# Hybrid attention and state-space layer, fp32 on one core: first tile of x in two column halves, last row tile's final product in two halves of 256 columns

## What is computed

```python
xn = rmsnorm(h, norm1_w[layer])
proj = xn @ w_in[layer]
...
h = h + mix.astype(h.dtype)
hn = rmsnorm(h, norm2_w[layer])
u = causal_dwconv(hn @ w_up[layer], ffn_conv_w[layer], ffn_conv_b[layer])
val, gt = _split(u, (D_FF, D_FF))
h = h + ((jax.nn.silu(gt) * val) @ w_down[layer]).astype(h.dtype)
return rmsnorm(h, final_norm_w)
```

## Time and profile before

| what | us |
|---|---|
| median of 3 runs | 1033.05 |
| lowest, highest | 1031.88, 1033.41 |
| the profiled execution | 1032.09 |
| its span, first to last instruction | 1030.4 |
| PE busy in it | 1020.3 |
| PEld busy | 832.3 |
| DVE busy | 642.4 |
| ACT busy | 465.9 |
| POOL busy | 93.6 |

### The profile page before, as it was taken

One profiled execution on the slowest core, in us unless ns is written; L12 is line 12 of the kernel. 1 busy time (PEld: TensorE's weight loads), 2 busy tenths in 40 slices (PEclk: granted clock), 3 DMA queues, 4 the chain that ended last, 5 costly groups with the idle time before them and its releaser, 6 DMA issues.

```text
span 1030.4 us, 13442 instructions
## 1 busy us (share of the span) xinstructions
PE 1020.3 (99%) x5095; PEld 832.3 (81%) x5095; DVE 642.4 (62%) x897; ACT 465.9 (45%) x834; POOL 93.6 (9%) x128
## 2 busy tenths in 40 slices
PE   9999999999999999999999999999999999999997
PEld 8887777777888888888888888898888888888886
DVE  7637998684476686895754544566766676641332
ACT  6335556455555636765633222444444444331233
POOL 0001111110222120122220100000000000000000
PEclk9999999999999999999999999999999999999999
DMA  7622221224656424555362743223332223232222
GB/s 218 123 85 82 82 69 55 83 82 114 160 122 168 130 84 128 141 128 150 102 211 83 253 156 104 80 83 104 100 119 85 81 84 120 89 129 89 93 71 81
DMA packets 123499, 116.49 MB, mean 113 GB/s; under 512 B 21342, under 2 KB 111782, under 8 KB 123447
## 3 DMA queue, kind: packets, MB, share of 16 engines
q1 hardware_dynamic: 95509, 94.74, 29.9%
q10 hardware_dynamic: 25346, 12.59, 5.3%
q0 software_dynamic: 2592, 8.46, 2.2%
HBM read 109.41 MB, written 6.36 MB: 112 GB/s over the span
## 4 chain that ended last, share of the span: by engine, by line
PE 87%; DVE 9%; ACT 2%; issue 1%; DMA 0%; SPq 0%; DVEq 0%; ACTq 0%
PE banks L1270 27%; PE banks L1271 26%; PE banks L1272 26%; DVE conv_acc L1218 3%; DVE w_lo L871 1%; PE banks L1375 1%; PE banks L1368 1%; ACT probs L622 1%; PE banks L1363 1%; PE banks L1343 1%; PE banks L1351 1%; DVE probs L963 1%; DVE small L949 0%; DVE scores L946 0%; DMA w_raw<-in_w_in 0%
## 5 line engine op out<-in xcount | busy, mean ns | idle before, releaser
L871 DVE TENSOR_TENSOR w_lo<-w_raw,w_hi 128x1024 fp32r<-128x1024 f32 (+1 forms) x166 | 201.4, 1253 | 124.0 <-ACT w_hi L584 122.8
L584 ACT ACTIVATE w_hi<-w_raw 128x1024 fp32r<-128x1024 f32 (+1 forms) x166 | 164.1, 1037 | 108.9 <-PE banks L1272 107.6
L1270 PE MATMUL banks<-xn_hi,w_hi 128*128 128x512 f32 x528 | 211.8, 401 | 0.0
L1271 PE MATMUL banks<-xn_lo,w_hi 128*128 128x512 f32 x528 | 206.1, 390 | 0.0
L1272 PE MATMUL banks<-xn_hi,w_lo 128*128 128x512 f32 x528 | 206.0, 390 | 0.0
L1270 PE MATMUL banks<-hn_hi,w_hi 128*128 128x512 f32 (+1 forms) x376 | 141.3, 376 | 0.0
L1271 PE MATMUL banks<-hn_lo,w_hi 128*128 128x512 f32 (+1 forms) x376 | 141.2, 375 | 0.0
L1272 PE MATMUL banks<-hn_hi,w_lo 128*128 128x512 f32 (+1 forms) x376 | 141.2, 375 | 0.0
L1270 PEld LDWEIGHTS banks<-xn_hi,w_hi 128*128 128x128 f32 x528 | 99.1, 188 | 29.8 <-issue 9.3
L1272 PEld LDWEIGHTS banks<-xn_hi,w_lo 128*128 128x128 f32 x528 | 99.1, 188 | 21.6
L1271 PEld LDWEIGHTS banks<-xn_lo,w_hi 128*128 128x128 f32 x528 | 99.3, 188 | 18.9
(11 more groups left out here) (222 smaller groups left out, 1460.0 us busy)
## 6 DMA issues: line engine op xcount, KB each, us to landing
w_raw<-in_w_in SPq DMA_DIRECT2D x29, 1024.0 KB, 5.4
w_raw<-in_w_up SPq DMA_DIRECT2D x22, 1024.0 KB, 5.0
decay<-acs_scratch ACTq DMA_DIRECT2D x16, 512.0 KB, 6.1
w_raw<-in_w_ssd_o SPq DMA_DIRECT2D x8, 1024.0 KB, 5.3
w_raw<-in_w_down SPq DMA_DIRECT2D x8, 1024.0 KB, 5.0
w_raw<-in_w_in SPq DMA_DIRECT2D x16, 256.0 KB, 4.6
w_raw<-in_w_attn_o SPq DMA_DIRECT2D x16, 256.0 KB, 4.6
decay_off<-acs_scratch ACTq DMA_DIRECT2D x32, 128.0 KB, 3.7
```

What stands on the lines that cost most here:

```text
L584: A.activation(whi[:, c % 2, lo_:hi_], raw[:, c % 2, lo_:hi_], ACT.Copy).then_inc(w_rounded, 1)
L871: V.tensor_tensor(wlo[:, c % 2, lo_:hi_], raw[:, c % 2, lo_:hi_], f32(whi[:, c % 2, lo_:hi_]), ALU.subtract).then_inc(w_split, 1)
L1270: T.matmul(out_, w[0], m[0], start=first, stop=False)
L1271: T.matmul(out_, w[0], m[1], start=False, stop=False)
```

## The change

Four things are done.

- **x.** The load of row tile 0 becomes two DMAs on SP, columns 0 to 511 and columns 512 to 1023, each with its own semaphore. ScalarE squares the left half when it is there, turns its sum into a bias with an Identity (sum / 1024 + eps), squares the right half, and takes the root with that bias (`square_x0`).
- **The last row tile on TensorE.** For `down`, the sum of row tile 3 over all chunks but the last is closed with chunk 10. VectorE adds it to `h` then (`f_early`). The last chunk's product for row tile 3 is made apart, as 12 matmuls of 256 columns into bank 4 and 12 into bank 5, with a semaphore behind each.
- **The last row tile on VectorE and ScalarE.** `last_quarter(k)` adds one quarter (256 columns) to `h` and multiplies it by the final weights into `fo`. ScalarE squares each quarter by itself. The first quarter's sum goes into a bias (`fpart[:, 1]`) by a small VectorE instruction. At the end VectorE multiplies columns 256 to 1023 of `fo` by the reciprocal root in one `tensor_scalar`, ScalarE columns 0 to 255.
- **The last stores.** ScalarE issues the store of columns 0 to 255 itself, SP that of columns 256 to 1023.

The diff, without the lines that only create semaphores and move small columns:

```diff
@@ sync
                 for t in ((0,), (1, 2, 3))[c] if c < 2 else ():
+                    if t == 0:
+                        eng.dma_start(xnat[:, 0, 0:512], x[0, 0:P, 0:512]).then_inc(x_left_in, 16)
+                        eng.dma_start(xnat[:, 0, 512:D], x[0, 0:P, 512:D]).then_inc(x_in[0], 16)
+                        continue
                     eng.dma_start(xnat[:, t, :], x[0, t * P:(t + 1) * P, :]).then_inc(x_in[t], 16)
...
-                for nh in range(2) if t == NT - 1 else (slice(0, 2),):
-                    if t < NT - 1 or nh == 0:
-                        eng.wait_ge(f_left, t + 1)
-                    if t < NT - 1 or nh == 1:
-                        eng.wait_ge(f_right, t + 1)
-                    cols = slice(0, D) if t < NT - 1 else slice(nh * 512, nh * 512 + 512)
-                    eng.dma_start(out[0, t * P:(t + 1) * P, cols], fo[:, t, cols]).then_inc(f_st, 16)
+                if t < NT - 1:
+                    eng.wait_ge(f_left, t + 1)
+                eng.wait_ge(f_right, t + 1)
+                cols = slice(0, D) if t < NT - 1 else slice(256, D)
+                eng.dma_start(out[0, t * P:(t + 1) * P, cols], fo[:, t, cols]).then_inc(f_st, 16)
@@ scalar, start
+            def square_x0():
+
+                left, bias = small[:, 169:170], small[:, 170:171]
+                eng.wait_ge(x_left_in, 16)
+                A.activation(junk[:, 0:512], xnat[:, 0, 0:512], ACT.Square, accum_out=left).then_inc(n_left, 1)
+                eng.wait_ge(n_left, 1)
+                A.activation(bias, left, ACT.Identity, bias=epsc, scale=1.0 / D).then_inc(n_left, 1)
+                eng.wait_ge(x_in[0], 16)
+                A.activation(junk[:, 512:D], xnat[:, 0, 512:D], ACT.Square, accum_out=ss[:, 0:1]).then_inc(n_sq, 1)
+                eng.wait_ge(n_left, 2)
+                eng.wait_ge(n_sq, 1)
+                A.activation(sd[:, 0:1], ss[:, 0:1], ACT.Sqrt, bias=bias, scale=1.0 / D).then_inc(n_sd, 1)
...
-            square_x(0)
+            square_x0()
@@ scalar, end
                 eng.wait_ge(f_sq, NT + t)
+                if t == NT - 1:
+                    A.activation(fjunk[:, 0:256], h[:, t, 512:768], ACT.Square, accum_out=fss[:, t:t + 1]).then_inc(f_sq, 1)
+                    eng.wait_ge(dn_add, NT + t + 2)
+                    A.activation(fjunk[:, 256:512], h[:, t, 768:D], ACT.Square, accum_out=fpart[:, 0:1]).then_inc(f_sq, 1)
+                    eng.wait_ge(f_sq, NT + t + 2)
+                    eng.wait_ge(f_part, 1)
+                    A.activation(fsd[:, t:t + 1], fpart[:, 0:1], ACT.Sqrt, bias=fpart[:, 1:2], scale=1.0 / D).then_inc(f_sd, 1)
+                    eng.wait_ge(f_rs, t + 1)
+                    eng.wait_ge(f_pre, NT)
+                    A.activation(fo[:, t, 0:256], fo[:, t, 0:256], ACT.Identity, scale=frs[:, t:t + 1]).then_inc(f_left, 1)
+                    eng.wait_ge(f_left, NT)
+                    eng.dma_start(out[0, t * P:(t + 1) * P, 0:256], fo[:, t, 0:256]).then_inc(f_st, 16)
+                    break
@@ vector
             def final_right(t):
 
                 eng.wait_ge(f_rs, t + 1)
+                if t == NT - 1:
+                    eng.wait_ge(f_pre, NT + 2)
+                    V.tensor_scalar(fo[:, t, 256:D], fo[:, t, 256:D], frs[:, t:t + 1], None, ALU.mult).then_inc(f_right, 1)
+                    return
...
+            def last_quarter(k, t=NT - 1):
+
+                cols = slice(512 + 256 * k, 768 + 256 * k)
+                if k == 0:
+                    eng.wait_ge(f_early, 1)
+                V.tensor_tensor(h[:, t, cols], h[:, t, cols], PS[:, 4 + k, 256 * k:256 * k + 256], ALU.add).then_inc(dn_add, 1)
+                eng.wait_ge(dn_add, NT + t + 1 + k)
+                V.tensor_tensor(fo[:, t, cols], h[:, t, cols], fnw[:, cols], ALU.mult).then_inc(f_pre, 1)
+                if k == 0:
+                    eng.wait_ge(f_sq, NT + t + 1)
+                    V.scalar_tensor_tensor(out=fpart[:, 1:2], in0=fss[:, t:t + 1], scalar=1.0 / D, in1=fhb[:, t:t + 1],
+                                           op0=ALU.mult, op1=ALU.add).then_inc(f_part, 1)
...
+                if kind == "down" and i == 10:
+                    eng.wait_ge(gemm_done, DONE[c, NT - 1])
+                    V.tensor_tensor(h[:, NT - 1, 512:D], h[:, NT - 1, 512:D], PS[:, NT - 1, :], ALU.add).then_inc(f_early, 1)
...
+                            if kind == "down" and nh == 1 and t == NT - 1:
+                                last_quarter(0)
+                                final_right(t - 1)
+                                eng.wait_ge(gemm_done, DONE[c, t] + 1)
+                                last_quarter(1)
+                                eng.wait_ge(f_sd, t + 1)
+                                V.reciprocal(frs[:, t:t + 1], fsd[:, t:t + 1]).then_inc(f_rs, 1)
+                                break
@@ tensor
+                            ends = last and not (kind == "down" and t == NT - 1) or kind == "down" and (i, t) in ((5, NT - 1), (10, NT - 1))
+                            if kind == "down" and i == 11 and t == NT - 1:
+                                take(4, dn_add, NT)
+                                take(5, dn_add, NT)
+                                for n0 in (0, 256):
+                                    for kt in range(nk):
+                                        cols_ = slice(kt * width + n0, kt * width + n0 + 256)
+                                        ins = three(PS[:, 4 + n0 // 256, n0:n0 + 256], (mh[:, kb + kt, tok], ml[:, kb + kt, tok]),
+                                                    (whi[:, c % 2, cols_], wlo[:, c % 2, cols_]), kt == 0, kt == nk - 1)
+                                    ins.then_inc(gemm_done, 1)
+                                continue
```

More of the change, by code:

```diff
@@ L287, in hybrid_layer @@
         fss, fsd, frs = small[:, 80:84], small[:, 84:88], small[:, 88:92]
-        gsd, grs = small[:, 172:176], small[:, 176:180]
+        gsd, grs = small[:, 174:178], small[:, 178:182]
         fhs, fhb = small[:, 160:164], small[:, 164:168]
         acs = small[:, 192:192 + NT * NH]
+        fpart = small[:, 171:173]
         hss, hsd, hrs = small[:, 92:96], small[:, 96:100], small[:, 100:104]
@@ L315, in hybrid_layer @@
         n1_in, n2_in, n1_spread = sem("norm1_in"), sem("norm2_in"), sem("norm1_spread")
+        x_left_in, n_left = sem("x_left_in0"), sem("n_left_squared")
         n1_copy, n1_pad = sem("norm1_copied"), sem("norm1_padded")
@@ L355, in hybrid_layer @@
         dn_add = sem("down_added")
-        f_sq, f_sd, f_rs, f_pre, f_left, f_right, fnw_in = [sem("final_" + s) for s in (
-            "squared", "root", "rstd", "left_weighted", "left_out", "right_out", "row_in")]
+        f_sq, f_sd, f_rs, f_pre, f_left, f_right, f_part, f_early, fnw_in = [sem("final_" + s) for s in (
+            "squared", "root", "rstd", "left_weighted", "left_out", "right_out", "part_biased", "summed_but_last", "row_in")]
         f_st, f_bias = sem("final_stored"), sem("final_first_half")
@@ L1524, in _ @@
                                             (whi[:, ck % 2, cols_], wlo[:, ck % 2, cols_]),
-                                            first and ck == cs[0] and kt == 0, last and ck == c and kt == nk - 1)
+                                            first and ck == cs[0] and kt == 0, ends and ck == c and kt == nk - 1)
                             ins.then_inc(gemm_done, 1)
```

## The result

| | before | changed |
|---|---|---|
| median of 22 runs each, us | 1032.70 | 1033.93 |
| lowest to highest, us | 1031.84 to 1033.41 | 1033.44 to 1035.95 |
| profiled execution, us | 1032.09 | 1033.75 |
| its span, us | 1030.4 | 1032.0 |

The medians differ by 1.23 us. The ratio is 1.0016, with a 95% interval of 1.0011 to 1.0022: 1.1 to 2.3 us slower, 1.65 in the middle. The middle is within 0.2%, as forecast, and the time is inside the range, but the loss is real: the interval leaves out a ratio of 1, and I had summed to 0.45 us. Three of the 22 executions are at 1035.4 to 1036.0; the mean of the other 19 is 1.3 us above the mean before. More on the three at the end.

A forecast was written before the change was run, and what follows sets the result against it. TensorE bounds the kernel for 87% of the span; the change edits only head and tail. Head 0.05 plus tail 0.40 on the profiled 1032.09 gives 1032.54, plus 0.96 to the median makes 1033.5 us, range 1032.2 to 1034.8.

The forecast's parts named there:

- the shape of the whole: Head, TensorE stretch, tail: a microsecond in the head passes through one for one; the tail counts by itself.
- The early add of everything but the last chunk: VectorE, about 1013.7 us: one 512-wide add, covered by 10.09 us of idle time; costs nothing, uncovered 0.61.
- the tail's chain: VectorE and ScalarE, row tile 3: halving takes 0.48 us off, late start adds 1.25; last products 0.77 later.
- The 768-wide product: VectorE's last product, tensor times a column: twice the rate, 0.61 us; at the single rate 1.01.
- The wait for ScalarE's square: VectorE waits until 1024.97, tile 2's right product queued behind; last quarter's add starts 1025.75, not 1024.66.
- Rival A: Tail: the last quarter is not held up; chain gains 0.5 to 0.8, stores pass about 0.2; 1032.9 us; chance 0.12.
- C: TensorE's last 24 matmuls: halves no faster than whole ones, step 0.23 instead of 0.12; 1035.0 us; chance 0.04.
- the stores: Tail's end: the last store lands 0.32 to 0.56 us late; 0.40 taken.
- Bounds: 0 and 0.45; I take 0.05: Head: how much later the first weights land because SP issues them 0.45 us later; 0.05 us taken.
- the issue is covered by that backlog: Head: DMA engines at 0.92 from 1.6 to 6.4 us, weights queued behind x, so their later issue is covered.
- B: Head late: weights' landing follows SP's issue, 0.45 later, 0.85 with tail; or x's halves land together; 1033.9 to 1034.3; chance 0.19.
- 0.05 + 0.40: The forecast's sum: 0.05 us for the head plus 0.40 for the tail, 0.45 us slower.

The follow-up runs named there:

- the reordered tail: Kernel before plus the change's tail, x whole, VectorE's last-quarter add moved ahead of the small instruction's wait and both weights products: 1032.06 us, ratio 0.9997.
- the tail alone: The changed kernel with row tile 0 of x loaded and squared whole again, against the kernel before: 1033.10 us, ratio 1.0005.
- the head alone: The kernel before with only the change's two x loads and `square_x0`, nothing of its tail: 1033.28 us, ratio 1.0012.
- the 8 KB load: The kernel before with one small parameter load issued on SP between x and the first weights: 1033.20 us, ratio 1.0014.
- the small load behind: The kernel before with one 8 KB parameter load issued directly behind the first weights, ahead of x's row tiles 1 to 3: 1032.55 us, ratio 1.0000.
- the reordered tail with the small part by ACT: The reordered tail, with the first weights' 64 KB load issued on ACT's queue instead of SP's, against the kernel before: 1035.41 us, ratio 1.0026.
- more warming matmuls: The changed kernel with 12 instead of 4 small matmuls on `ones` ahead of TensorE's first products: 1034.48 us, ratio 1.0019 to the kernel before.

## Why the prediction came out as it did

**Right: the shape of the whole.** Head and tail add within the noise, and TensorE's stretch between them passed the head's delay on whole (1.01 at the first product, 1.10 at row tile 2's reciprocal). The early add of everything but the last chunk cost nothing that shows.

**Right: the tail's chain.** In the changed kernel's profile, shifted by the 1.10 that the head adds, the sum put the last add at 1026.85 (measured 1026.78), the root at 1027.85 (1027.77), the last products at 1028.38 (1028.29) and ACT's issue at 1028.91 (1028.83). The 768-wide product was put at 0.61 and took 0.62, so the double rate stood. The wait for ScalarE's square, with two things queued behind it, was named as the cause, and the reordered tail shows it to be one: without it the last add comes 0.84 earlier. Rival A, that the quarter is not held up, falls for the change as it is made; it describes the reordered tail instead. C falls with the step of 0.12.

**A little off: the stores.** I took 0.40 between bounds of 0.32 and 0.56. The last landing, 2.3 us behind SP's last issue where it was 1.9, makes the tail about 0.5 in the changed kernel's profile; the tail alone has 0.47 by its profile and 0.5 by its ratio.

**Wrong: "Bounds: 0 and 0.45; I take 0.05".** This is the step that failed. It measured 1.01 in the profiled execution and 1.2 (0.3 to 2.2) for the head alone. It holds two errors. The first is "the issue is covered by that backlog". I read a DMA share of 0.92 over 4.8 us as a backlog that a later issue could hide in. One more load ahead of the weights made them late, and the 8 KB load shows it without a byte of x. A high share is no proof of cover: the changed kernel has 0.94 at 3.4 to 4.2 us, and its weights were late. The second is the upper bound. I let the landing be at most as late as the issue. In the profiled execution the middle ones of the 32 increments did stay within it, at 5.89 where they had come at 5.5, but the last came 1.01 later, and ScalarE waits for the last. In the head alone SP's issue itself took 1.12 in place of 0.43, so the begin of the issue was no measure of its end. B had the right place and direction, that the landing follows SP's queue. It stood at a chance of 0.19 where it deserved the larger part, and at less than half of its price. Its condition, that the weights' data does not queue behind x, is seen in the profiles with a dry stretch and not in that of the changed kernel.

The Trainium skill (DMA: Bandwidth & Descriptors, Rules for kernel authors) says that two transfers to disjoint partition halves serialize on the same engines and that one is to be preferred. The traces agree for two halves of the columns: by the landing records the right half came at 4.62 in the changed kernel and the whole x at 4.21 before. Over the profiles with either way of loading x on SP's queue it is 4.3 to 4.6 for the right half and 4.2 to 4.5 for the whole. So the split brought x as a whole no earlier, and the first weights behind it came later.

**Why the class held all the same.** 0.05 + 0.40 should have been about 1.0 + 0.5. Both stand under 0.2% of 1033 us, so no change was the answer with either. The median was 0.43 above my 1033.5, and this nearness is partly luck. By the medians I was 0.78 short (0.45 for 1.23), and 0.35 of that was hidden because the kernel before came out at 1032.70 in the comparison, where the three runs that I started from had 1033.05.

**Open.** In the changed kernel's profile an issue 0.47 later becomes a landing 1.01 later, without a slow issue: the chain has it from 1.74 to 2.17. The landing is then 5.2 behind the issue's end, against 4.7 before, 4.4 in the tail alone and 4.9 with the small load behind. The middle ones of its 32 increments are 0.4 later than before, about what the later issue is worth. The other 0.6 is in the last increments, which straggle: the third from last came at 6.56, the last at 7.39, where before it was 5.90 and 6.38. No run tells what an engine waits for there.

## What to carry to other kernels

A high busy share of the DMA engines does not prove that a load is covered: put one small load ahead of it, and one behind it, and see which moves the end. In a prologue, do not price an extra issue ahead of the first load that compute waits for at its own 0.45 us alone (here it cost about 1 us), and ask which load it pushes back before asking what it brings. And where an engine's program has a wait for another engine, put ahead of it everything that is ready: by the profiles the same instructions in another order were worth 0.8 us here.

## What the runs showed of the hardware

**An early issue on SP can take 1.1 us or more.** SP's third load issue took 1.12 in the head alone and 1.18 with the small load ahead, and there it was that of the first weights, so they were late. In the tail alone SP's second and third issue together took 1.74, where they take 0.97 before:

```profile
1.27 0.42 SPq L472
...
1.74 4.37 DMA w_raw<-in_w_in
```

By this chain the second took 0.42, so the slow one was again the third, there the 64 KB part, and it did no harm: the weights came at 6.11. It does not come in every execution (the changed kernel's profile has 0.98 for two). What it waits for was not found.

**TensorE's clock after an idle start.** With the small load ahead of the weights TensorE had nothing to do for 2.23 us before its first product. A little later the granted clock was 0.50, its 1.2 GHz level:

```profile
12.00:13.00 1.00, 1.00 (x6) 1.00 (x5) 0.96 (x4) 1.00 (x2) 0.00 (x0) 0.50 1.15 297
```

The matmuls there have a step of 0.24, as the rows at 13.24 and 13.48 show, where the same ones have 0.14 in the changed kernel's profile (10.66, 10.80), which had been idle for 1.27 us. That execution's span is 1033.9, 3.5 above before: 1.98 of it is the later first product (11.39 against 9.41), and the other 1.5 fit this stretch, where the granted clock was below 1.00 in the slices from 11 to 15 us. A late load in the head can so cost more than its lateness.

As long an idle time did not do it elsewhere. In the profile of the reordered tail with the small part by ACT, TensorE stood idle for longer, and the clock stayed at 1.00 (the next matmuls are at 12.48 and 12.62, again a step of 0.14):

```profile
12.24 0.40 PE L1330 MATMUL banks<-vd_w_hi,xn_hi 128*128 128x288 f32 x1 [2.42 <-DVE xn_lo L1121]
```

Whether the three slowest executions of the change had such a stretch was not seen, since none of them was profiled. Their mean granted clocks point to it: 0.996, 0.996 and 0.997, where the other 19 have 0.998 or 0.999. The slowest of the head alone (1035.65) has 0.997, and the execution with the small load ahead that is shown here has 0.997 too. With more warming matmuls none of 11 is below 0.998, but they cost 0.5 us in the median (1034.48 against 1033.93, in separate comparisons).
